# Decoder trunk on one core: the strip of gate columns goes behind the delta-rule projections, and the first delta-rule unit is split between x's tiles

## The reference, cut to what matters

```
h    = rmsnorm(x, g_mix)
proj = h @ w_in      # columns: gla q|k|v | r | code (16) | gdn pre-conv q|k|v (3072) | z (1024) | a (8) | b (8)
xc   = concatenate([conv_buf, cqkv]);  conv = silu(sum_j xc[:, j:j+T] * gdn_conv_w[j])   # 4 taps
gate_pre = code @ gla_w_gate2 + gla_b_gate ;  beta = sigmoid(b) ;  g = -exp(a_log) * softplus(a + dt_bias)
... (gated linear attention and gated delta rule, their gates, w_out, cross attention, SwiGLU, final norm)
```

## Time and profile before

| | us |
|---|---|
| median of 3 executions | 1779.99 (1779.85 to 1781.88) |
| the profiled execution | 1779.38 |
| its span in the profile | 1777.7 |
| PE busy | 1753.1 (99% of the span) |
| DVE, ACT, POOL busy | 1078.1, 761.8, 173.2 |

### The profile page before, as it was taken

How to read it: one execution, slowest core, us unless ns; L and a number is a source line. 1 busy time by engine, 2 the same in 40 slices (tenths; PEclk the granted TensorE clock), 3 DMA queues, 4 the chain that set the end, 5 groups by cost and what they waited for, 6 DMA issues and landing times.

```text
span 1777.7 us, 35497 instructions
## 1 busy us (share of the span) xinstructions
PE 1753.1 (99%) x14527; PEld 1676.6 (94%) x14527; DVE 1078.1 (61%) x1502; ACT 761.8 (43%) x801; POOL 173.2 (10%) x170
## 2 busy tenths in 40 slices
PE   8999999999999999999999999999999999999997
PEld 6999999988999998886799999999999999999997
DVE  6778447746676776653376666665444666655444
ACT  6554546445733433433323444443333444443444
POOL 4000001001055000000035200000000000000231
PEclk9999999999999999999999999999999999999999
DMA  8555645561566679778846788885557988874553
GB/s 274 163 173 188 189 143 174 164 208 48 176 214 197 207 270 330 257 269 316 281 131 198 198 258 251 246 234 140 179 168 222 248 248 246 244 212 129 177 181 114
DMA packets 414556, 367.26 MB, mean 207 GB/s; under 512 B 11455, under 2 KB 373950, under 8 KB 413910
## 3 DMA queue, kind: packets, MB, share of 16 engines
q1 hardware_dynamic: 386792, 340.76, 62.4%
q10 hardware_dynamic: 27678, 25.26, 4.4%
HBM read 347.84 MB, written 18.35 MB: 206 GB/s over the span
## 4 chain that ended last, share of the span: by engine, by line
PE 95%; DVE 2%; DMA 1%; ACT 1%; issue 0%; DVEq 0%; SPq 0%; ACTq 0%
PE ps L479 72%; PE ps L575 10%; PE ps L556 4%; PE ps L542 1%; PE ps L1025 1%; PE ps L1554 1%; DMA gst<-in_state_gla_dram 1%; PE ps L1565 1%; PE ps L1519 1%; DVE act_lo L2282 0%; PE ps L1496 0%; PE ps L1094 0%; DVE w_lo L458 0%; PE ps L1310 0%; DVE act_hi L2281 0%; PE ps L1151 0%
## 5 line engine op out<-in xcount | busy, mean ns | idle before, releaser
L451 ACT ACTIVATE w_hi<-raw 128x2048 fp32r<-128x2048 f32 (+1 forms) x284 | 510.4, 1797 | 893.4 <-PE ps L479 723.6
L458 DVE TENSOR_TENSOR w_lo<-raw,w_hi 128x2048 fp32r<-128x2048 f32 (+1 forms) x284 | 619.3, 2180 | 296.2 <-ACT w_hi L451 294.9
L479 PE MATMUL ps<-act_hi,w_lo 128*128 128x264 f32 x2560 | 732.3, 286 | 1.0 <-DVE cst L2310 0.5
L479 PE MATMUL ps<-act_lo,w_hi 128*128 128x264 f32 x2560 | 725.6, 283 | 0.0
L479 PE MATMUL ps<-act_hi,w_hi 128*128 128x264 f32 x2560 | 725.2, 283 | 0.0
L479 PEld LDWEIGHTS ps<-act_hi,w_lo 128*128 128x128 f32 x2560 | 482.3, 188 | 3.4 <-issue 1.6
L479 PEld LDWEIGHTS ps<-act_lo,w_hi 128*128 128x128 f32 x2560 | 482.7, 189 | 0.4
L479 PEld LDWEIGHTS ps<-act_hi,w_hi 128*128 128x128 f32 x2560 | 480.1, 188 | 0.0
L479 PE MATMUL ps<-ff_hi,w_lo 128*128 128x264 f32 x704 | 201.2, 286 | 0.0
L479 PE MATMUL ps<-ff_hi,w_hi 128*128 128x264 f32 x704 | 200.2, 284 | 0.0
L479 PE MATMUL ps<-ff_lo,w_hi 128*128 128x264 f32 x704 | 199.5, 283 | 0.0
(11 more groups left out here) (455 smaller groups left out, 1932.6 us busy)
## 6 DMA issues: line engine op xcount, KB each, us to landing
raw<-in_w_in_dram SPq DMA_DIRECT2D x56, 1024.0 KB, 7.5
raw<-in_ffn_w_gate_dram SPq DMA_DIRECT2D x44, 1024.0 KB, 5.8
raw<-in_ffn_w_up_dram SPq DMA_DIRECT2D x44, 1024.0 KB, 5.9
raw<-in_ffn_w_down_dram SPq DMA_DIRECT2D x32, 768.0 KB, 4.9
raw<-in_ffn_w_down_dram SPq DMA_DIRECT2D x32, 640.0 KB, 6.1
raw<-in_w_out_dram SPq DMA_DIRECT2D x16, 1024.0 KB, 6.3
raw<-in_xa_w_q_dram SPq DMA_DIRECT2D x16, 1024.0 KB, 7.1
raw<-in_xa_w_k_dram SPq DMA_DIRECT2D x16, 1024.0 KB, 7.4
```

The lines of the kernel that those rows point to most:

```text
L451: act.activation(w_part(ph, w_hi[b]), raw_part(ph, r, half), ACT.Copy)\
L458: dve.tensor_tensor(w_part(ph, w_lo[b]), raw_part(ph, r, half), w_part(ph, w_hi[b]), ALU.subtract)\
L479: mm = pe.matmul(ps[:, acc(ph, u), 0:ph.cols], w[b][:, k, :], v[:, kk + k, 0:ph.cols], start=first and k == 0 and m == 0, stop=last and k ...
```

## The change

The strip becomes the unit behind the 24 gdn units (slot 12, unit 24), and the first gdn unit takes its place at the start. SP loads `crows` ahead of the first weights. On PE all conv state turns now stand together behind tile 14's turn; tile 15 is turned within the first gdn unit; the sum of squares is run in the middle of the second one. ACT splits gdn units 0 and 1 before x's tiles 8 and 12 and copies the conv state out of PSUM itself; DVE splits unit 0 before tile 11. The first four gdn units are written out: on ACT the split of unit 3 stands behind the take of unit 0.

```
 def plan():
-    runs = [("strip", 1, KT), ("gdn", 12, KT), ("gla", 8, KT), ...
+    runs = [("gdn", 12, KT), ("strip", 1, KT), ("gla", 8, KT), ...
 load():
-            sp.wait_ge(lo_split, 2 * s + (0 if by_half else 1))
+            sp.wait_ge(lo_split, 2 * s + (2 if ph.name in ("gdn", "strip") else 0 if by_half else 1))
 SP:
-            load(sp, PH["strip"], 0, 0)
             sp.dma_start(crows[:, :], ...).then_inc(crows_landed, 16)
+            load(sp, PH["gdn"], 0, 0)
...
-            for j in range(2):
-                load(sp, PH["gdn"], 0, j)
+            load(sp, PH["gdn"], 0, 1)
             sp.wait_ge(x_ready, KT)
             sp.dma_start(x_keep[:, :], ...)
             (gdn slots from the third on)
+            load(sp, PH["strip"], 0, 0)
             sp.wait_ge(xrows_landed, 32 + 16)
             sp.wait_ge(ssq_ready, KT)
             sp.dma_start(w2[:, :], G2[0]).then_inc(scalars_landed, 16)
+            sp.wait_ge(lo_split, PH["strip"].u0 + LO_CREDIT)
             stream("gla")
 PE:
-            for k in range(KT):
-                turn_rows(k)
-                (k == 9: turns of grows, cwrows; k >= 10: four turn_conv each)
-            for k in range(KT):
-                strip_products(k)
-            pe.wait_ge(x_ready, KT)
-            sum_squares(1, TT)
-            pe.wait_ge(cols_ready, 2)
-            for u in range(4):
-                products(pe, ph, 0, u, act_hi, act_lo)
+            for k in range(KT - 1):
+                turn_rows(k)
+            (turns of grows, cwrows, then all 24 turn_conv)
+            def tile_in(k):
+                if k == 2:
+                    turn_rows(KT - 1)
+                pe.wait_ge(x_taken, k + 1)
+            products(pe, ph, 0, 0, act_hi, act_lo, ready=tile_in)
+            pe.wait_ge(cols_ready, 3)
+            products(pe, ph, 0, 1, act_hi, act_lo, middle=lambda: sum_squares(1, TT))
+            for u in (2, 3):
                 products(pe, ph, 0, u, act_hi, act_lo)
             (gdn units 4 to 23)
+            products(pe, PH["strip"], 0, 0, act_hi, act_lo)
 ACT:
             for k in range(KT):
-                if k == 10:
-                    split(PH["strip"], 0, 0)
+                if k == 8:
+                    split(PH["gdn"], 0, 0)
+                if k == 12:
+                    act.wait_ge(consts_ready, 1)
+                    split(PH["gdn"], 0, 1)
                 (x kept and squared)
-            split(PH["gdn"], 0, 0)
-            split(PH["gdn"], 0, 1)
+            act.wait_ge(cols_turned, 2)
+            (conv state out of PSUM, two copies).then_inc(cols_ready, 1)
+            split(ph, 0, 2)
             rms(1, TT, D)
-            run("gdn", gdn_take, "gla")
+            for u in range(4):
+                if u:
+                    split(ph, u // 2, (u + 2) % 4)
+                gdn_take(ph, 0, u)
+            run("gdn", gdn_take, "strip", first=1)
+            split(PH["gla"], 0, 1)
 DVE:
                 if k == 11:
-                    split(PH["strip"], 0, 0)
+                    split(PH["gdn"], 0, 0)
...
-            split(PH["gdn"], 0, 0)
             dve.wait_ge(cols_turned, 2)
             (small copies; the two of the conv state are gone)
+            split(ph, 0, 1)
+            split(ph, 0, 2)
+            dve.wait_ge(cols_ready, 3)
             dve.wait_ge(rstd_ready, 1)
-            (take of the strip)
-            run("gdn", gdn, "gla")
+            for u in range(4):
+                gdn(ph, 0, u)
+                if u:
+                    split(ph, u // 2, (u + 2) % 4)
+            run("gdn", gdn, "strip", first=1)
+            (take of the strip)
+            split(PH["gla"], 0, 1)
```

More of the change, by code:

```diff
@@ L87, in plan @@
 def plan():
-    runs = [("strip", 1, KT), ("gdn", 12, KT), ("gla", 8, KT), ("r", 4, KT), ("z", 4, KT), ("w_out", 8, KT), ("x_q", 8, KT),
+    runs = [("gdn", 12, KT), ("strip", 1, KT), ("gla", 8, KT), ("r", 4, KT), ("z", 4, KT), ("w_out", 8, KT), ("x_q", 8, KT),
             ("mem_k", 8, KT), ("mem_v", 8, KT), ("x_o", 8, KT), ("gu0", HALF_K, KT), ("dn0", 16, DK_),
@@ L1045, in turn_rows @@
                 turn(ps[:, W4 + k % 4, T:TT], xsrow[:, k * P:(k + 1) * P]).then_inc(x_turned, 1)
[L1047 to L1057, removed]
@@ L1059, in turn_conv @@
             def turn_conv(t):
                 return turn(ps[:, 2 + t // 12, (t % 12) * 24:(t % 12) * 24 + 24], crows[:, t * P:(t + 1) * P])
-            ph = PH["strip"]
-            for k in range(KT):
+            ph = PH["gdn"]
+            for k in range(KT - 1):
                 turn_rows(k)
[L1066 to L1074, removed]
@@ L1075, in _ @@
-            mm.then_inc(cols_turned, 1)
-            for k in range(KT):
-                strip_products(k)
-            pe.wait_ge(x_ready, KT)
-            sum_squares(1, TT)
-            pe.wait_ge(cols_ready, 2)
-            ph = PH["gdn"]
-            for u in range(4):
+            pe.wait_ge(cols_ready, 1)
+            pe.wait_ge(rows_landed, 16 * 8)
+            turn(ps[:, 1, P:P + 87 - KT], grows[:, :])
+            turn(ps[:, 1, 2 * P:2 * P + CW * CT], cwrows[:, :])
+            pe.wait_ge(crows_landed, 16)
@@ L1083, in _ @@
+            for t in range(CT):
+                mm = turn_conv(t)
+            mm.then_inc(cols_turned, 1)
+            def tile_in(k):
[6 more added lines that the diff above has]
+            for u in (2, 3):
                 products(pe, ph, 0, u, act_hi, act_lo)
@@ L1806, in run_with_pieces, with run @@
                     take(ph, i, u)
-            def run(name, take, nxt, before=None):
+            def run(name, take, nxt, before=None, first=0):
                 ph = PH[name]
-                with act.Fori(0, ph.loops - 1) as i:
+                with act.Fori(first, ph.loops - 1) as i:
                     for u in range(4):
@@ L1822, in run @@
                         split(ph, i, u + 2)
+                    elif nxt == "strip":
+                        split(PH["strip" if u == 2 else "gla"], 0, 0)
                     elif nxt is not None:
@@ L1843, in _ @@
                 act.activation(xsq[:, k % 4, :], x[:, k, :], ACT.Square).then_inc(sq_ready, 1)
-            split(PH["gdn"], 0, 0)
-            act.wait_ge(consts_ready, 1)
-            split(PH["gdn"], 0, 1)
-            rms(1, TT, D)
-            run("gdn", gdn_take, "gla")
+            act.wait_ge(cols_turned, 2)
+            for m in range(2):
+                ins = act.activation(cst[:, 12 * m:12 * m + 12, :].rearrange("p t (j b) -> p t b j", j=3),
+                                     ps[:, 2 + m, 0:288].rearrange("p (t b j) -> p t b j", t=12, j=3), ACT.Copy)
+            ins.then_inc(cols_ready, 1)
+            ph = PH["gdn"]
+            split(ph, 0, 2)
+            rms(1, TT, D)
+            for u in range(4):
[4 more added lines that the diff above has]
+            split(PH["gla"], 0, 1)
             c1 = consts[:, 1:2]
@@ L2260, in split, with run @@
                 split_lo(dve, ph, i, u)
-            def run(name, take, nxt):
+            def run(name, take, nxt, first=0):
                 ph = PH[name]
-                with dve.Fori(0, ph.loops - 1) as i:
+                with dve.Fori(first, ph.loops - 1) as i:
                     for u in range(4):
@@ L2301, in _ @@
                 if k == 11:
-                    split(PH["strip"], 0, 0)
+                    split(PH["gdn"], 0, 0)
                 dve.wait_ge(x_turned, k + 1)
                 halves_of(k, ps[:, W4 + k % 4, 0:TT], GAIN_MIX, act_hi, act_lo, x_taken)
-            split(PH["gdn"], 0, 0)
             dve.wait_ge(cols_turned, 2)
             dve.tensor_copy(cols[:, KT:87], ps[:, 1, P:P + 87 - KT])
[L2308 to L2314, removed]
+            dve.tensor_copy(convw[:, :], ps[:, 1, 2 * P:2 * P + CW * CT]).then_inc(cols_ready, 1)
+            ph = PH["gdn"]
+            split(ph, 0, 1)
+            split(ph, 0, 2)
+            dve.wait_ge(cols_ready, 3)
             dve.wait_ge(rstd_ready, 1)
             dve.wait_ge(consts_ready, 2)
-            tile_wait(dve, PH["strip"], 0, 0)
-            dve.tensor_tensor(strip[:, :], ps[:, 0, 0:TT], rstd[:, :], ALU.mult).then_inc(acc_free, 1)
-            run("gdn", gdn, "gla")
+            for u in range(4):
[3 more added lines that the diff above has]
+            run("gdn", gdn, "strip", first=1)
+            ph = PH["strip"]
+            tile_wait(dve, ph, 0, 0)
+            dve.tensor_tensor(strip[:, :], out_of(ph, 0), rstd[:, :], ALU.mult).then_inc(acc_free, 1)
+            split(PH["gla"], 0, 1)
             def b3(v, n):
```

## The result

The changed kernel takes 1782.13 us, the median of 12 executions (1781.02 to 1786.81), against 1780.01 for the kernel before in the same job (12 executions, 1776.97 to 1782.06): ratio 1.002, with a 95% interval of 1.0012 to 1.0028. The profiled execution of the changed kernel took 1782.03 us (span 1780.3), that of before 1779.38.

The account below looks back on a forecast made before the run. PE, busy 99% of the span, bounds the kernel, so only its waits count: 2.7 us ahead of the fourth gdn unit plus 0.2 us for the strip's place make 2.9 us, 1782.9 us forecast, range 1780.9 to 1784.9.

Parts of the forecast that it names:

- The rival without a stall: Fourth gdn unit: ACT's chain 2.7 us shorter, so it starts at 45.2 without idle PE; 1780.2 us, chance 0.07.
- One sign that I had named for a wrong forecast: Anywhere on PE: an idle stretch of over 1 us, elsewhere than ahead of the fourth gdn unit, that before lacks.
- The start of the products: First products on PE: start at about 24.9 us instead of 25.15, with the first slot needed by 16.5.
- Unit 0: First gdn unit on PE: 7.35 us as the strip had, plus 0.8 for tile 15's turn, 8.2 us.
- The bound "0.4 more": First gdn unit: 0.4 us more if the slow stretch is longer by half of tile 15's turn.
- quick start: Rival, first gdn unit: takes 5.81 + 0.8 us, so all comes 1.5 us earlier; 1781.4 us, chance 0.08.
- The chain: From the sum of squares over ACT and DVE to the fourth gdn unit: 11.3 us, leaving PE idle 2.7 us.
- The Ln load: ACT, ahead of the first `rstd`: Ln's table load (1.28 us) lies beside the wait for the sum of squares.
- The rival of 1.28 us: ACT: Ln's table load comes behind its wait, fourth gdn unit 1.28 us later; 1784.2 us, chance 0.27.
- The slow level after the stall: Rival, PE after the idle stretch: matmuls again 0.22 us apart, costing 1.5 us; 1784.4 us, chance 0.08.
- The strip's new place: Ahead of the first gla unit: its slot is needed one unit after its buffer is free; 0.2 us wait.
- The sum: Whole kernel: 2.7 us for the stall plus 0.2 for the strip's new place, 2.9 us slower, median 1782.9 us.

Follow-up runs that it names:

- the mended kernel: Changed kernel with unit 3 split ahead of take 0, conv turns ahead of tile 12, first slot ahead of `crows`, first gla slot by columns: 1776.00 and 1776.06 us.
- the kernel with all of x: Kernel before, delayed at the start by DVE writing zeros into all of x before ACT fills it: ratio 1.0025.

## Why the prediction was right, and where two errors met

- **The bound and the mechanism.** Right. PE has no break in its chain but the two named: the idle stretch ahead of the fourth gdn unit, ended by DVE's low part (2.33 us; forecast 2.7), and the one ahead of the first gla unit (0.35; forecast 0.2). The rival without a stall fell with it. One sign that I had named for a wrong forecast did come: an idle stretch of over 1 us that before doesn't have stands elsewhere, 2.27 us ahead of the turn of tile 12 (19.71), while PE waits for ACT, which is splitting unit 0. Part of it lay unnamed in my own sum, where ACT keeps tile 8 only at 18.4 + 0.4 = 18.8 and PE is through with tile 11 at 17.4; the late slot added the rest. It works through the start of the products, and moving the conv state's turns into it was worth 2.6 us there.
- **The start of the products.** 25.33 for 24.9. The term that failed is the landing of the first slot: the split began at 17.47, 0.97 later than the 16.5 of the sum and outside the 15.5 to 17 that I expected. I had priced each 0.1 us of it at 0.1 us; 0.4 arrived, since the 24 conv turns took 2.7 us and not 3.2. The run with the slot ahead of `crows` took half of the wait away, by an earlier issue.
- **Unit 0.** Forecast 8.2 us. The sum of squares stands at 37.19, half a unit (2.9) behind unit 1's start at 34.3, so unit 0 took 9.0. The slow distance lasted from 25.33 to 31.0, 5.7 us, where the strip had 3.2 (25.15 to 28.4). Less the turn of tile 15 (0.8), that is 1.65 us more of slow matmuls, and 1 - 0.12/0.22 of it is 0.75 lost. The bound "0.4 more" was too small: over all runs of this study the stretch lasted 3.2 to 6.1 us, for the mended kernel, profiled twice, 5.7 and 4.6, and for the changed one 5.7 and 5.3. The 3.2 us of the one profile of before is the shortest of the 14, and the four kernels that start as before does have 4.7 to 6.1. So that the change lengthens the stretch is not shown: the 0.75 us can be how these two profiles fell out, and taking one profile's 7.35 us as the price of the first unit was the error. No "quick start" was seen in any.
- **The chain.** From the start of Ln to the fourth unit 48.83 - 37.83 = 11.0 us for 11.3. Each link is within 0.25 of its term: Ln to DVE 2.31 (2.25), DVE's taps to the tail 2.46 (2.7), tail to SiLU's end 1.94 (1.96), split and low part with their steps 4.29 (4.4).
- **The Ln load.** Beside the wait, as taken: it begins at 36.50, right behind the split, and is through at 37.78, while the sum ends at 37.80. The rival of 1.28 us fell. The Trainium skill (ScalarE: Activation LUTs, Table sets: the hidden batching unit) has Ln and Exp in one set; here the loads are at 36.50 and 38.33, 1.28 us each, so the measurement decides against its one load, and the run without Exp shows that the second was on the path.
- **The slow level after the stall.** Not in the changed kernel's profile: after 2.33 us of idle time the matmuls stand 0.13 us apart (49.02, 49.15). In the run with the first slot ahead of `crows` the same wait was followed by the 0.50 clock. The rule that I cited from the Trainium skill (TensorE: Matmul & The Clock Gate, Part 1), that an idle TensorE falls back to 1.2 GHz, agrees with that one trace, where even so the first 1.3 us ran quick, and the other four profiles that have this wait of 2.33 us show no fall; one of five is too few to price the rival by.
- **The strip's new place.** 0.6 us for 0.2. The wait is 0.37 (177.02 against 48.83 + 22 x 5.81 = 176.65), with a landing of 7.79 as I took it, but 0.9 us from the low part's end (163.95) to the DMA's start, not 0.7. In the chain the first unit after the wait takes 6.08 us instead of 5.81; that 0.27 I had not counted, and it stands in every run that has the wait. Its matmuls are no slower: the first stands 0.23 from the second (177.02, 177.25) and the rest 0.12 apart, as at 33.59 in the kernel before. So 0.11 of it is the restart, and the rest is how the chain books the end of the matmul ahead of a wait, whose row is longer than its distance. From start to start the wait costs 0.63 - 0.12 = 0.5 and the restart 0.1 us.
- **The sum.** By the mark the steps gave 3.6 + 0.6 = 4.2 us, where I forecast 2.9. The steps were 1.3 us too small, in the first slot and unit 0 (1.2 together), the strip's place (0.4), less 0.3 from the chain. The step that fails beside these is the one from the mark to the median, which I had taken as one to one. It holds for the fastest executions (+4.1), while the median rose by 2.1, since executions of before are seldom its fastest; the stretches at 0.50 behind the mark are what sets them apart. So the number 1782.9 came near 1782.13 partly because two errors met, which was luck. The causes of the 2.9 us were right in kind and 70% of the size.

## What to carry to other kernels

When a result that gates the first tile of a pipeline is moved later, look at what stands behind its consumer in the order of the engine: here a ready 1.9 us split queued behind a take that waited for `rstd`, and PE stood for 2.3 us; putting the ready work ahead of the wait took all of it back. Work that PE can do without the busy engine (the conv state's turns) belongs where PE waits for that engine, not in a block behind it. And where a shift of a few us is judged, read a mark in the trace and the fastest executions beside the median: here the medians moved by up to 2.3 us less than the fastest executions did.

## What the runs showed of the hardware that was not expected

- Slow stretches of TensorE in mid-kernel, at a granted clock of 0.50 for about 3 us (451.9 to 455 in the profile of before, 1.6 us lost) and up to 10.2 us (444.8 to 455.0 in the kernel with all of x), in some executions of a kernel and not in others: the mean granted clock of the executions of before goes from 0.995 to 0.998.
- In the slow stretch behind the first product, with 264 columns 0.22 us apart, the granted clock column reads 1.00 (26 to 30 us, before and after). At 49 us in the run with the slot ahead of `crows` it reads 0.50 for the same distance. The clock entries of a trace begin only where the matmuls become quick (at 28.3 us before, at 31.0 after), so the 1.00 ahead of that is no measurement. The distance of matmuls is what to go by.
- The first slot of 2 MB was there at 17.4, though it was issued at 2.74 to 5.8: its transfer took 14.1 us, where one in the gla phase took 7.8. With the 24 rows of the conv state behind it instead of ahead it was issued 0.55 us earlier and was there at 16.9.
- Ahead of the second slot, SP needs 5.52 us to issue one small DMA (timeline of SP, changed kernel):

```profile
2.74 3.06 SPq L427 DMA_DIRECT2D raw<-in_w_in_dram  x2
5.84 5.52 SPq L766 DMA_DIRECT2D dtb<-in_gdn_dt_bias_dram  x1
```
